# Hybrid sparse and stick-breaking attention block: another layout of the first transfers, roundings and warm-up products

## The reference

```
h  = RMSNorm(x, g_pre_mix)
qa,ka,va | q_idx,k_idx,w_idx | qb,kb,vb | gate_a,gate_b = h @ w_in
score[t,s] = sum_h w_idx[t,h] * relu(q_idx[t,h] . k_idx[s] / 8) / sqrt(8)   (block-causal in chunks of 64)
o_a = softmax attention of qa on the 128 best keys of each token, with a T5 position bias
o_b = stick-breaking attention of qb, kb, vb (strictly causal)
m  = sigmoid(gate_a) * (o_a @ w_branch_sparse) + sigmoid(gate_b) * (o_b @ w_branch_sb)
x  = x + RMSNorm(m @ w_out, g_post_mix)
x  = x + RMSNorm(SwiGLU(RMSNorm(x, g_pre_ffn) @ w_gate_up) @ w_down, g_post_ffn)
```

## Time and profile before

| | us |
|---|---|
| three runs | 782.69, 782.78, 783.38 (median 782.78) |
| profiled execution, its own time | 782.44 |
| its span, first to last instruction | 780.6 |
| TensorE busy | 772.0 (99% of the span) |
| GpSimd busy | 411.6 |
| VectorE busy | 375.1 |
| ScalarE busy | 349.4 |

### The profile page before, as it was taken

How to read it: one execution, slowest core, us unless ns; L and a number is a source line. 1 busy time by engine, 2 the same in 40 slices (tenths; PEclk the granted TensorE clock), 3 DMA queues, 4 the chain that set the end, 5 groups by cost and what they waited for, 6 DMA issues and landing times.

```text
span 780.6 us, 10435 instructions
## 1 busy us (share of the span) xinstructions
PE 772.0 (99%) x3667; PEld 646.9 (83%) x3667; DVE 375.1 (48%) x532; ACT 349.4 (45%) x558; POOL 411.6 (53%) x250
## 2 busy tenths in 40 slices
PE   9999999999999999999999999999999999999997
PEld 8788888888888888888879988888888888888885
DVE  4879959997566664399045000000000011444564
ACT  5662287776677766441365222222222222232243
POOL 6916366767588696234650343434444344443462
PEclk9999999999999999999999999999999999999999
DMA  9643441231224223122581132333323333123312
GB/s 339 181 143 98 145 122 55 69 95 54 62 62 114 70 60 109 55 88 74 195 263 55 55 105 69 95 107 107 99 68 101 107 107 101 65 104 107 107 54 109
DMA packets 102441, 81.50 MB, mean 104 GB/s; under 512 B 3200, under 2 KB 91272, under 8 KB 102408
## 3 DMA queue, kind: packets, MB, share of 16 engines
q1 hardware_dynamic: 102216, 81.06, 33.5%
q10 hardware_dynamic: 192, 0.01, 0.0%
HBM read 76.85 MB, written 3.68 MB: 103 GB/s over the span
## 4 chain that ended last, share of the span: by engine, by line
PE 90%; DVE 5%; DMA 2%; ACT 2%; issue 1%; POOL 0%; SPq 0%; DVEq 0%; POOLq 0%; ACTq 0%
PE ps L497 22%; PE ps L476 18%; PE ps L478 18%; PE ps L477 18%; PE ps L562 3%; PE ps L715 2%; PE ps L704 2%; DMA raw<-in_w_gate_up 1%; PE ps L687 1%; PE ps L689 1%; DVE keep_buf L1529 1%; PE ps L517 1%; ACT y_buf L855 1%; DVE e_buf L1537 1%; PE ps L609 1%
## 5 line engine op out<-in xcount | busy, mean ns | idle before, releaser
L1200 POOL TENSOR_TENSOR w_lo<-raw,w_hi 128x1024 fp32r<-128x1024 f32 x74 | 177.0, 2393 | 247.7 <-ACT w_hi L826 218.7
L476 PE MATMUL ps<-h_hi,w_hi 128*128 128x512 f32 (+1 forms) x608 | 236.0, 388 | 0.0
L478 PE MATMUL ps<-h_hi,w_lo 128*128 128x512 f32 (+1 forms) x608 | 234.0, 385 | 0.0
L477 PE MATMUL ps<-h_lo,w_hi 128*128 128x512 f32 (+1 forms) x608 | 233.9, 385 | 0.0
L826 ACT ACTIVATE w_hi<-raw 128x1024 fp32r<-128x1024 f32 (+1 forms) x70 | 74.3, 1061 | 271.2 <-PE ps L478 192.0
L478 PEld LDWEIGHTS ps<-h_hi,w_lo 128*128 128x128 f32 x608 | 114.3, 188 | 22.5
L476 PEld LDWEIGHTS ps<-h_hi,w_hi 128*128 128x128 f32 x608 | 114.4, 188 | 21.3 <-issue 0.3
L477 PEld LDWEIGHTS ps<-h_lo,w_hi 128*128 128x128 f32 x608 | 114.5, 188 | 20.9
L1679 DVE TENSOR_TENSOR act<-silu,ps 128x512 f32 (+1 forms) x22 | 15.1, 688 | 211.3 <-PE ps L478 211.3
L1308 POOL TENSOR_TENSOR w_lo<-raw,w_hi 128x1024 fp32r<-128x1024 f32 x30 | 77.4, 2582 | 30.7 <-ACT w_hi L974 30.3
L1684 DVE TENSOR_TENSOR d_lo<-act,d_hi 128x512 fp32r<-128x512 f32 x18 | 43.0, 2396 | 51.6 <-ACT d_hi L1137 51.6
(11 more groups left out here) (218 smaller groups left out, 1321.5 us busy)
## 6 DMA issues: line engine op xcount, KB each, us to landing
raw<-in_w_gate_up SPq DMA_DIRECT2D x44, 512.0 KB, 4.5
raw<-in_w_in SPq DMA_DIRECT2D x40, 512.0 KB, 4.3
raw<-in_w_down SPq DMA_DIRECT2D x22, 512.0 KB, 4.0
raw<-in_w_out SPq DMA_DIRECT2D x8, 512.0 KB, 4.1
x_t<-in_first SPq DMA_DIRECT2D x8, 256.0 KB, 7.0
wq_raw<-in_first SPq DMA_DIRECT2D x8, 256.0 KB, 6.2
x_in<-in_x SPq DMA_DIRECT2D x4, 512.0 KB, 7.0
qi_twice<-qi_hi SPq DMA_DIRECT2D x16, 128.0 KB, 2.3
```

What stands on the lines that cost most here:

```text
L476: mm(acc, whi_c, a_hi_, start=first, stop=False)
L477: mm(acc, whi_c, a_lo_, start=False, stop=False)
L478: return mm(acc, wlo_c, a_hi_, start=False, stop=last)
L1200: nc.gpsimd.tensor_tensor(w_lo[:, at(u), :], raw[:, at((d % 2) * 2 + u), :], w_hi[:, at(u), :], sub).then_inc(w_lo_done, 1)
```

## The change

The gain columns no longer have a transfer of their own. The host puts them in front of chunk 0 of x, in an array `head` of 128 x 520, which goes into a buffer `x_first` of its own as the first transfer on SyncE's queue. Chunk 0 of the weights goes on ScalarE's queue instead of SyncE's. The bias table moves from ScalarE's queue to SyncE's, behind chunk 1. Chunk 0 of x is rounded by two engines: ScalarE takes columns 0 to 319, VectorE 320 to 511. VectorE rounds chunk 0 of the weights in two halves, and TensorE waits for the second half only before its third product. VectorE then copies the gain columns to `g_cols`, for which ScalarE waits before chunk 1. `WARM` is 7 instead of 9.

```diff
-WARM = 9
+WARM = 7
+X_ACT = 320
...
+    top[0] = 4 * (KC + 6) * S
+    x_first = sb("x_first", KC + S)
...
-        chunk_in(0)
+        sp.dma_start(x_first[:, :], head).then_inc(x_t_in[0], 16)
         chunk_in(1)
+        sp.dma_start(rel_in_rows[:, :], rel_bias).then_inc(small_in, 16)
         rows_in(0)
...
         def first_pass(w, act, c, first, last):
             for j in range(PAIRS):
+                if first and j == PAIRS // 2:
+                    pe.wait_ge(wq_hi_early_done, 1)
                 ins = mm(bank(j), w[:, c, j * P:(j + 1) * P], act[:, c, :], start=first, stop=last)
...
-            pe.wait_ge(*((wq_hi_done, c - TB) if c > TB else (wq_hi_early_done, c + 1)))
+            if c == 0:
+                pe.wait_ge(xg_part_done, 1)
+                pe.wait_ge(wq_part_done, 1)
+            else:
+                pe.wait_ge(*((wq_hi_done, c - TB) if c > TB else (wq_hi_early_done, c + 1)))
...
         def round_x(c):
             sc.wait_ge(x_t_in[c], 16)
+            if c == 1:
+                sc.wait_ge(g_kept, 1)
...
-        sc.dma_start(g_cols[:, :], gain_cols).then_inc(g_cols_in, 16)
-        sc.dma_start(rel_in_rows[:, :], rel_bias).then_inc(small_in, 16)
+        sc.dma_start(wq_raw[:, 0, :], first[0, :, S:2 * S]).then_inc(wq_in[0], 16)
         nc.scalar.preload_act_table(ACT.Sqrt)
         sc.sem_inc(acc_free, PAIRS)
-        sc.wait_ge(g_cols_in, 16)
-        round_x(0)
+        sc.wait_ge(x_t_in[0], 16)
+        run(xg_hi[:, 0, 0:X_ACT], x_first[:, KC:KC + X_ACT], ACT.Copy, scale=x_first[:, 0:1]).then_inc(xg_hi_done, 1)
...
         def rest_wq(c):
+            if c == 0:
+                gp.wait_ge(wq_part_done, 1)
...
-        for c in range(TB):
-            if c:
-                rest_x(c - 1)
+        ve.wait_ge(x_t_in[0], 16)
+        ts(xg_hi[:, 0, X_ACT:S], x_first[:, KC + X_ACT:KC + S], x_first[:, 0:1], None, ALU.mult).then_inc(xg_part_done, 1)
+        ve.wait_ge(wq_in[0], 16)
+        half = W // 2
+        nc.vector.tensor_copy(wq_hi[:, 0, 0:half], wq_raw[:, 0, 0:half]).then_inc(wq_part_done, 1)
+        nc.vector.tensor_copy(wq_hi[:, 0, half:W], wq_raw[:, 0, half:W]).then_inc(wq_hi_early_done, 1)
+        nc.vector.tensor_copy(g_cols[:, :], x_first[:, 0:KC]).then_inc(g_kept, 1)
+        ve.wait_ge(xg_part_done, 1)
+        ve.wait_ge(g_kept, 1)
+        for c in range(1, TB):
+            rest_x(c - 1)
             round_wq(c)
```

More of the change, by code:

```diff
@@ L121, in bias_runs, with build @@
     return runs
-def build(nc, first, gain_cols, first_kw, x, w_in, w_branch_sparse, w_branch_sb, w_out, w_gate_up, w_down,
+def build(nc, first, head, first_kw, x, w_in, w_branch_sparse, w_branch_sb, w_out, w_gate_up, w_down,
           g_pre_mix, g_post_mix, g_pre_ffn, g_post_ffn, rel_bias, out):
@@ L208, in build @@
     wq_hi, wq_lo = sb("wq_hi", [KC, S], F32R), sb("wq_lo", [KC, S], F32R)
+    top[0] = 4 * (KC + 6) * S
+    x_first = sb("x_first", KC + S)
+    assert top[0] <= 4 * 2 * KC * S
     top[0] = heads_out
@@ L265, in build @@
     x_in_got, x1_in = sems(*(f"x_in_got{t}" for t in range(TB))), sems(*(f"x1_in{t}" for t in range(TB)))
-    small_in, kw_in, g_cols_in = sems("small_in", "kw_in", "g_cols_in")
+    small_in, kw_in = sems("small_in", "kw_in")
+    g_kept, xg_part_done, wq_part_done = sems("g_kept", "xg_part_done", "wq_part_done")
     x_t_in, wq_in = sems(*(f"x_t_in{c}" for c in range(KC))), sems(*(f"wq_in{c}" for c in range(KC)))
@@ L1396, in _, with x_chunk @@
         ve.sem_inc(act_done, 2)
+        def x_chunk(c):
+            return x_t[:, c, :] if c else x_first[:, KC:KC + S]
         def rest_x(c):
             ve.wait_ge(xg_hi_done, c + 1)
-            stt(xg_lo[:, c, :], x_t[:, c, :], g_cols[:, c:c + 1], xg_hi[:, c, :], ALU.mult, sub).then_inc(xg_lo_done, 1)
+            stt(xg_lo[:, c, :], x_chunk(c), g_cols[:, c:c + 1], xg_hi[:, c, :], ALU.mult, sub).then_inc(xg_lo_done, 1)
         def make_h(c):
@@ L1404, in make_h @@
                 ve.wait_ge(xh_lo_done, c - 1)
-            stt(bank(4 + c % 2), x_t[:, c, :], g_cols[:, c:c + 1], bank(7), ALU.mult, ALU.mult).then_inc(xh_made, 1)
+            stt(bank(4 + c % 2), x_chunk(c), g_cols[:, c:c + 1], bank(7), ALU.mult, ALU.mult).then_inc(xh_made, 1)
         def rest_h(c):
@@ L1729 @@
     laid = {"first": np.concatenate([np.asarray(inputs["x"][0]).T, w[:, COL_QI:COL_QI + W]], axis=1).reshape(KC, P, 2 * S),
-            "gain_cols": np.asarray(inputs["g_pre_mix"][0]).reshape(KC, P).T,
+            "head": np.concatenate([np.asarray(inputs["g_pre_mix"][0]).reshape(KC, P).T, np.asarray(inputs["x"][0]).T[0:P]], axis=1),
             "first_kw": w[:, COL_KI:COL_KI + KW].reshape(KC, P, KW).transpose(1, 0, 2).reshape(P, KC * KW)}
```

## The result

| | kernel before | changed kernel |
|---|---|---|
| median of 22 runs | 782.37 us | 784.17 us |
| lowest and highest | 781.82 to 783.71 | 782.63 to 789.99 |
| profiled execution, span | 780.6 | 782.4 |

The changed kernel is slower by about a quarter of a percent: ratio 1.0027, 95% interval 1.0017 to 1.0036. The ratio is an estimate over the runs and not the quotient of the two medians, here and in the table of experiments. The forecast was 782.6 with a range to 783.8. Nineteen of the 22 runs lie between 782.6 and 784.9 and three near 789; both groups need a cause.

What follows compares the result with a forecast made beforehand. TensorE's queue of products, busy 99% of the span, was taken as the bound. A start 0.41 us earlier, discounted for the lower clock, gave -0.20 us: 782.78 - 0.20 = 782.58, said as 782.6, range 781.7 to 783.8.

Steps and rivals of the forecast that it cites:

- rival A: TensorE's clock rises later, each microsecond costing 0.49 us; a 3.79 us slip gives 784.4; chance 0.15.
- the start 0.41 us earlier: TensorE's first loads of chunk 0 start at 4.45 instead of 4.86 us, worth 0.20 us at the lower clock.
- x can land between 3.46 and 4.11: First transfers: chunk 0 of x lands within these times in us, taken as 3.85, both queues sharing full DMA engines.
- my outer bound of 5.0: Latest start of TensorE's first real loads, with x at 4.11 and both VectorE pieces at 0.43 us.
- the discount of A: Argument against a later clock rise: TensorE stays busy over 90% of the stretch before it, despite a 0.4 us pause.
- VectorE's remainder of x (0.75 us): In chunk 0 it takes 0.75 us, ends near 5.5 us and is wanted at 6.25.
- No wait: In chunk 0, the second weight half and both remainders are ready before TensorE wants them.
- the landing at 4.11: First weight transfer of the kernel before, landing at 4.11 us in the profiled trace.
- warm-up products, not data, release the first real product: Start of the kernel before: operands were ready 0.3 us before TensorE took them.
- ScalarE's 320 columns: Rounding of ScalarE's part of chunk 0 of x takes 0.55 us, ending at 4.40.
- VectorE's two pieces: Rounding VectorE's 192 columns of x and the first half of the weights in chunk 0, 0.25 us each.
- the cover of the later chunks: Tightest later operands, remainders in chunks 2 and 3, are ready 0.7 and 0.86 us early, so a 0.2 to 0.4 shift uncovers neither.

Runs made afterwards that it cites:

- e8: Kernel before with gain columns in front of x (2080-byte rows), x and first weights both on SyncE's queue, nine warm-ups: 782.49 us against 782.78 before.
- e11: Changed kernel with the first weights back on SyncE's queue behind x, seven warm-ups kept: 782.58 us against 782.68 for the kernel before.
- e1: Changed kernel with nine warm-up products instead of seven: 782.83 us against 782.85 for the kernel before.
- e5: Kernel before, nine warm-ups, its first product made to wait also for GpSimd's remainder of the weights: 784.39 us against 782.78 before.
- e9: Changed kernel with eleven warm-up products instead of seven: 783.03 us against 782.68 for the kernel before.
- e13: Changed kernel with its seven warm-ups started later, VectorE clearing an unused buffer first: 782.73 us against 782.47 for the kernel before.
- e4: Kernel before with only the new transfers (gain columns before x, weights on ScalarE's queue), one rounding engine each, nine warm-ups: 782.99 us against 782.85 before.
- e6: Kernel before with eleven warm-up products instead of nine: 782.62 us against 782.78 before.
- e3: Kernel before with only the shared rounding of chunk 0 and the split weight wait, nine warm-ups: 782.80 us against 782.85 before.
- e10: Changed kernel with both first transfers on SyncE's queue, ten warm-ups and VectorE's remainder of x first: 782.40 us against 782.68 for the kernel before.
- e7: Kernel before with 2048-byte x rows kept and first weights on ScalarE's queue behind the gain columns, nine warm-ups: 783.54 us against 782.78 before.
- e2: Kernel before with seven warm-up products instead of nine: 783.58 us against 782.85 before.
- e12: Changed kernel run again unaltered: 784.32 us against 782.68 for the kernel before.
- e14: Changed kernel with VectorE's remainder of x ahead of GpSimd's weight remainder and the gain-column copy: 783.47 us against 782.47 for the kernel before.
- e15: Changed kernel with GpSimd's small bias instructions moved behind the weight remainders: 783.79 us against 782.47 for the kernel before.

## Why the prediction was wrong

Where the end is set was right: TensorE's queue, whose start moves the whole kernel. So was the clock's part as a price: rival A put 0.49 us on each microsecond of later rise and 784.4 on a slip of 3.79; the rise slipped by about 3.5 us and the time is 784.17. It got a chance of 0.15. That its sum came so close is in part luck: it has the start 0.41 us earlier and no wait, where the start was 0.37 later, a wait cost 0.30, and 0.25 was made up after chunk 0.

The step that failed first is "x can land between 3.46 and 4.11". The upper end supposed that two queues move in sum what one does, and that chunk 1 takes nothing from x. They moved half in the stretch from 2 to 3 us, much of chunk 1 moved ahead of the end of x, x landed at 4.6, and with it the first load came at 5.27, beyond my outer bound of 5.0. e8 and e11 show that one queue would have kept x at 2.8 us after issue.

The second is the discount of A: "TensorE would still be busy for over 90% of the stretch before the rise". The pause was not 0.43 but 1.14 us, and the lower level lasted to about 10 us, not 6.7; that is 1.38 us, the largest term, which the forecast had at nothing. The medians of e1, e5, e9 and e13 tie the loss to the pause: nine warm-ups with one of 1.88 lose 1.6 us, part of it by the late start itself; seven without one lose 0.3, which is not clear of noise. Short pauses of 0.2 to 0.5 (e1, e4, e11) cost nothing that can be measured in the median. The discount was right for them, and e11's trace shows that even then the rise can be late.

The third is "VectorE's remainder of x (0.75 us)". It took 1.79, because GpSimd now started 0.04 us ahead of it, where before VectorE was ahead by 0.17. I had taken the duration of a row without the order in which the two engines start. "No wait" for chunk 0 fell with it: 0.30 us.

The fourth is a habit: the landing at 4.11 was read from one execution and used as fixed. Five traces with the same transfers have 4.11 to 5.13. Nine warm-ups were not the late end that they seemed; "warm-up products, not data, release the first real product" held for that execution and for e8's, whose data came as early, and not where they landed later. Right in detail were the 14 warm-up loads, which end near 4.1, ScalarE's 320 columns (0.56 against 0.55), VectorE's two pieces (0.32 and 0.29 against 0.25 each), and the cover of the later chunks in the profiled run. The executions near 789 were in no case of mine: beyond 0.2% on the slow side I had only A.

## What to carry to other kernels

Warm-up products should end after the latest usual landing of the operands, not after the one in the trace at hand: two products too many cost nothing here (e6), two too few with a landing 1.1 us later cost 1.6 to 1.8 us. Do not split the first two large transfers over two queues to start them together: here x landed 1.1 us later for it. Where VectorE and GpSimd subtract side by side, order them so that the one that TensorE waits for starts first. Whether gaps in GpSimd's stream prevent the rare slow executions is not shown. Read more than one execution before a margin of half a microsecond is built on a landing.

## What the runs showed of the hardware

- TensorE starts at its lower level, and how long that lasts depends on what it did before. With nine or more warm-ups from 1.07 us and a pause of at most 0.52 us, 188 ns loads begin between 5.5 and 7.6 us (before, e1, e3, e4, e6, e8, e9, e10), and in e7, whose pause was 1.36 us, already with the first real product at 6.34. With seven they begin between 10.3 and 10.8 us in the changed kernel, e2, e11 and e12, and near 9 us in e13, e14 and e15; with nine and a pause of 1.88 us (e5) at 10.3. The clock column prints 1.00 in all these stretches and tells nothing of the first low one. The Trainium skill (TensorE: Matmul & The Clock Gate, section What's actually happening) has the default as throttled and activity as what releases it. The traces agree with both: every one begins with 331 ns loads and changes to 188 ns after work.
- After a wait of 3.53 us in the middle of the work (e11) TensorE fell to 1.2 GHz for some three microseconds; four loads behind the wait still took 0.77 us together.
- A VectorE operation with two SBUF tensors, 0.74 us alone, takes 1.79 us when a GpSimd subtraction started just before it, and took 5.07 and 8.25 us in two stretches in which GpSimd had no gap. When VectorE starts first, GpSimd's 1.28 us become 1.71. The Trainium skill (GPSIMD Engine Reference, section 1, Specifications) lists the SBUF interfaces as shared with VectorE, with contention when its instruction has two SBUF inputs; the traces agree, and show besides how long one such wait can be.
- From 2 to 3 us, two transfers of 256 and 260 KB started together on two queues moved 147 to 194 GB/s (changed, e1, e4, e9, e12 to e15); with both on one queue it was 239 to 320 (before, e2, e3, e5, e6, e8, e10, e11). x landed 3.8 to 4.1 us after issue in the first case and 2.7 to 2.8 in the second. Which of the two, the rate or the order, costs x how much is not separated.
